# Where the causal mask of the attention scores is added, and how a column of scales is spread over a row: TensorE matmuls in place of a VectorE pass and of transposes

## The reference, cut to what matters

```python
def diff_attention(q, k, v, lam):
    for i in range(S // Q_BLOCK):                     # 8 blocks of 128 queries
        q0 = i * Q_BLOCK
        end = q0 + Q_BLOCK
        s = jnp.einsum('bqhcd,bkhcd->bhcqk', q[:, q0:end], k[:, :end]) * scale
        causal = kpos[None, :] <= qpos[:, None]
        p = jax.nn.softmax(jnp.where(causal, s, -jnp.inf), axis=-1)
        w = p[:, :, 0] - lam * p[:, :, 1]
        outs.append(jnp.einsum('bhqk,bkhe->bqhe', w, v[:, :end]))

def rmsnorm(x, g):
    y = x * lax.rsqrt(jnp.mean(x * x, axis=-1, keepdims=True) + NORM_EPS)
    return y * g
```

## Time and profile before

| what | value |
|---|---|
| median of 3 runs | 3637.75 us (3637.38 to 3641.05) |
| profiled execution, its own time | 3641.05 us |
| its span, first to last instruction | 3639.3 us |
| TensorE busy | 3379.2 us, 93% of the span |
| VectorE, ScalarE, GpSimd busy | 1452.7, 831.0 and 937.0 us |
| mean granted TensorE clock | 0.957 |
| attention with the head 0 projections left out | about 305 to 949 us of the span |
| dilated attention | about 1780 to 2370 us |

### The profile page before, as it was taken

How to read it: one execution, slowest core, us unless ns; L and a number is a source line. 1 busy time by engine, 2 the same in 40 slices (tenths; PEclk the granted TensorE clock), 3 DMA queues, 4 the chain that set the end, 5 groups by cost and what they waited for, 6 DMA issues and landing times.

```text
span 3639.3 us, 41501 instructions
## 1 busy us (share of the span) xinstructions
PE 3379.2 (93%) x15810; PEld 2742.8 (75%) x15810; DVE 1452.7 (40%) x1896; ACT 831.0 (23%) x1308; POOL 937.0 (26%) x514
## 2 busy tenths in 40 slices
PE   6989999998797898989999999889999989999999
PEld 5767777776685676768788888768787768888887
DVE  5653545455555666640021223222611542323231
ACT  4442333333201322221122222211201020101010
POOL 2222111110131221113222222234233323333332
PEclk9999999998898899979999999999999989999999
DMA  2110000000255012101211212231112111111112
GB/s 103 46 36 30 30 30 24 30 24 18 79 181 202 29 59 70 47 24 47 96 50 56 64 47 71 64 116 58 41 46 67 71 35 47 46 52 46 52 46 75
DMA packets 83698, 214.10 MB, mean 59 GB/s; under 512 B 7024, under 2 KB 33264, under 8 KB 83456
## 3 DMA queue, kind: packets, MB, share of 16 engines
q1 hardware_dynamic: 48176, 167.27, 14.1%
q10 hardware_dynamic: 35408, 45.24, 4.0%
HBM read 193.44 MB, written 19.04 MB: 58 GB/s over the span
## 4 chain that ended last, share of the span: by engine, by line
PE 80%; DVE 12%; ACT 3%; issue 3%; DMA 1%; PEld 1%; ACTq 0%; DVEq 0%; PEldq 0%; POOL 0%; SPq 0%; POOLq 0%
PE proj_bank L208 21%; PE proj_bank L210 20%; PE proj_bank L209 20%; PE aux_banks L208 2%; PE aux_banks L209 2%; PE aux_banks L210 2%; PE aux_banks L690 2%; PE aux_banks L1727 1%; ACT att_p L797 1%; PE aux_banks L699 1%; PE aux_banks L1410 1%; PE aux_banks L754 1%; DVE aux_banks L866 1%; PE aux_banks L1751 1%; PE aux_banks L495 1%
## 5 line engine op out<-in xcount | busy, mean ns | idle before, releaser
L208 PE MATMUL proj_bank<-h_hi,slab_hi 128*128 128x512 f32 x2816 | 1128.6, 401 | 41.9 <-ACT att_q L788 12.4
L209 PE MATMUL proj_bank<-h_lo,slab_hi 128*128 128x512 f32 x2816 | 1108.6, 394 | 0.0
L210 PE MATMUL proj_bank<-h_hi,slab_lo 128*128 128x512 f32 x2816 | 1108.6, 394 | 0.0
L226 POOL CAST slab_hi<-slab_raw 128x1024 fp32r<-128x1024 f32 x255 | 270.7, 1061 | 2659.7 <-PE proj_bank L210 2373.0
L228 POOL TENSOR_TENSOR slab_lo<-slab_raw,slab_hi 128x1024 fp32r<-128x1024 f32 x255 | 666.5, 2614 | 20.4
L208 PEld LDWEIGHTS proj_bank<-h_hi,slab_hi 128*128 128x128 f32 x2816 | 537.0, 191 | 168.3 <-issue 20.9
L210 PEld LDWEIGHTS proj_bank<-h_hi,slab_lo 128*128 128x128 f32 x2816 | 536.0, 190 | 115.2
L209 PEld LDWEIGHTS proj_bank<-h_lo,slab_hi 128*128 128x128 f32 x2816 | 537.2, 191 | 109.6 <-issue 2.2
L208 PE MATMUL proj_bank<-ffn_hi,slab_hi 128*128 128x512 f32 x512 | 199.2, 389 | 0.0
L209 PE MATMUL proj_bank<-ffn_lo,slab_hi 128*128 128x512 f32 x512 | 199.2, 389 | 0.0
L210 PE MATMUL proj_bank<-ffn_hi,slab_lo 128*128 128x512 f32 x512 | 199.2, 389 | 0.0
(11 more groups left out here) (329 smaller groups left out, 4099.2 us busy)
## 6 DMA issues: line engine op xcount, KB each, us to landing
slab_raw<-wts SPq DMA_DIRECT2D x255, 512.0 KB, 3.3
ada_w<-ada_w SPq DMA_DIRECT2D x64, 384.0 KB, 3.2
ssd_decay_rows<-decay_sums ACTq DMA_DIRECT2D x16, 512.0 KB, 4.2
dil_rows<-dilated_out ACTq DMA_DIRECT2D x12, 520.0 KB, 8.3
x_first<-xT SPq DMA_DIRECT2D x4, 1024.0 KB, 9.1
x_again<-xT ACTq DMA_DIRECT2D x4, 1024.0 KB, 8.1
x_kept<-x ACTq DMA_DIRECT2D x8, 512.0 KB, 4.3
mix_kept<-ssd_mix ACTq DMA_DIRECT2D x8, 512.0 KB, 7.7
```

The costliest lines, as they stand in the source:

```text
L208: pe.matmul(bank, k.whi[:, slot, wk, :], hi[:, xk, cols], start=first and a == 0, stop=False)
L209: pe.matmul(bank, k.whi[:, slot, wk, :], lo[:, xk, cols], start=False, stop=False)
L210: mm = pe.matmul(bank, k.wlo[:, slot, wk, :], hi[:, xk, cols], start=False, stop=last and a == len(ks) - 1)
L226: pool.tensor_copy(k.whi[:, slot], k.raw[:, slot]).then_inc(k.s_hi, 1)
```

## The change

Two edits. First, the mask is added by TensorE: behind each component's last score matmul a bfloat16 matmul of the identity with the 128x128 triangle accumulates into the same 128 columns, and `maxima` becomes one plain maximum over all keys for each component, each waiting for its own component only. Second, the spreads are no longer transposes but plain float32 matmuls with the same two operands. The mask operand shrinks to a bfloat16 copy of identity and triangle.

```diff
@@ make_core
-    k.mask = at("mask_row", 28.75, [P, MASK_W], BF16)
+    k.mask = at("mask_operands", 28.25, [P, 2, P], BF16)
@@ rstd_stage (line 282); the same edit in lines 717, 1148 and 1734
-            mm = pe.transpose(k.aux[:, bank0 + j // 4, (j % 4) * P:(j % 4 + 1) * P],
-                              k.rstd[:, j:j + 1].to_broadcast([P, P]), k.ident)
+            mm = pe.matmul(k.aux[:, bank0 + j // 4, (j % 4) * P:(j % 4 + 1) * P],
+                           k.rstd[:, j:j + 1].to_broadcast([P, P]), k.ident, start=True, stop=True)
@@ vectors_stage
-        dve.memset(k.mask[:, 0:MASK_W - P], 0.0)
-        dve.tensor_copy(k.mask[:, MASK_W - P:], k.causal)
+        dve.tensor_copy(k.mask.rearrange("p a b -> p (a b)"), k.const[:, IDENT:CAUSAL + P])
@@ attention_stage
-    mx = k.small[:, 64:68]
+    mx = k.small[:, 64:66]
@@ scores
-                mm = pe.matmul(own, q, kt[rows, par, i * P:keys], start=True, stop=True)
+                pe.matmul(own, q, kt[rows, par, i * P:keys], start=True, stop=False)
+                mm = pe.matmul(own, k.mask[:, 0], k.mask[:, 1], start=False, stop=True)
@@ maxima
-            early = max(0, keys - MASK_W)
             flat = score.rearrange("p (c a) b -> p c (a b)", c=2)
-            if early:
-                dve.wait_ge(s_score, step * 2 + 2)
-                v.settle(dve, dve.tensor_reduce(mx[:, 0:2], flat[:, :, 0:early], AX, ALU.max))
-                dve.sem_inc(s_seen, 1)
             for c in range(2):
-                if not early:
-                    dve.wait_ge(s_score, step * 2 + (c + 1))
-                    dve.sem_inc(s_seen, 1)
-                own = flat[:, c, early:keys]
-                ins = dve.tensor_tensor_reduce(own, own, k.mask[:, MASK_W - (keys - early):], 1.0, mx[:, c:c + 1] if early else LOWEST,
-                                               ALU.add, ALU.max, mx[:, 2 + c:3 + c])
+                dve.wait_ge(s_score, step * 2 + (c + 1))
+                ins = dve.tensor_reduce(mx[:, c:c + 1], flat[:, c, 0:keys], AX, ALU.max)
             v.settle(dve, ins)
-            dve.tensor_scalar(nmax, mx[:, 2:4], -SCALE, None, ALU.mult).then_inc(s_nmax, 1)
+            dve.tensor_scalar(nmax, mx, -SCALE, None, ALU.mult).then_inc(s_nmax, 1)
```

More of the change, by code:

```diff
@@ L28 @@
 NEG = -1e30
-LOWEST = -3e38
-MASK_W = 5 * 128
 ADA = 6 * D
@@ L123, in at @@
     def at(name, kb, shape, dt=F32):
-        size = (2 if dt == BF16 else 4) * int(np.prod(shape[1:]))
+        size = 4 * int(np.prod(shape[1:]))
         assert kb * 1024 + size <= k.top, (name, kb, size)
@@ L620, in attention_stage @@
     nmax, total, inv, lr = (k.small[:, 48 + 4 * i:50 + 4 * i] for i in range(4))
-    mx = k.small[:, 64:68]
+    mx = k.small[:, 64:66]
     score, turn, out = k.aux[:, 0:4, :], k.aux[:, 4, :], k.aux[:, 5, :]
     s_evac = k.sem("att_evacuated")
-    s_score, s_seen = k.sem("att_scored"), k.sem("att_scores_seen")
+    s_score = k.sem("att_scored")
     s_nmax = k.sem("att_max")
@@ L716, in spread @@
             for j in range(4):
-                mm = pe.transpose(turn[:, j * P:(j + 1) * P], k.rstd[:, 4 * a + j:4 * a + j + 1].to_broadcast([P, P]), k.ident)
+                mm = pe.matmul(turn[:, j * P:(j + 1) * P], k.rstd[:, 4 * a + j:4 * a + j + 1].to_broadcast([P, P]),
+                               k.ident, start=True, stop=True)
             mm.then_inc(s_turned, 1)
@@ L944, in _ @@
         with dve.Fori(0, (HEADS - 2) // 2) as m:
-            v.enter(m, 2 * (TT * 4 + 3))
+            v.enter(m, 2 * TT * 4)
             for b in range(2):
@@ L1147, in _ @@
             for j in range(TT):
-                mm = pe.transpose(k.aux[:, 2 * g + j // 4, (j % 4) * P:(j % 4 + 1) * P],
-                                  rstd[:, g * TT + j:g * TT + j + 1].to_broadcast([P, P]), k.ident)
+                mm = pe.matmul(k.aux[:, 2 * g + j // 4, (j % 4) * P:(j % 4 + 1) * P],
+                               rstd[:, g * TT + j:g * TT + j + 1].to_broadcast([P, P]), k.ident, start=True, stop=True)
             mm.then_inc(s_b, 1)
@@ L1733, in spread @@
             for b in range(TT):
-                mm = pe.transpose(spread_banks[:, b * P:(b + 1) * P], rstd[:, TT + b:TT + b + 1].to_broadcast([P, P]), k.ident)
+                mm = pe.matmul(spread_banks[:, b * P:(b + 1) * P], rstd[:, TT + b:TT + b + 1].to_broadcast([P, P]), k.ident, start=True, stop=True)
             mm.then_inc(s_spread, 1)
```

## The result

The changed kernel takes 3702.53 us (median of 4 runs, 3698.24 to 3704.24) against 3639.4 us of the kernel before in the same comparison: ratio 1.017, 95% interval 1.0152 to 1.0187. It is slower by about 63 us; the forecast was 3647.0, range 3636 to 3660. Its profiled execution took 3699.84 us and has a span of 3698.0 us, 58.7 more than before.

What follows compares the result with a forecast made beforehand. TensorE, busy for 93% of the span, was taken as the bound. Terms 10.8 + 5.5 + 0.9 - 5.8 - 2.1 = +9.3 us on the median 3637.75 gave 3647.0, range 3636 to 3660.

Steps and rivals of the forecast that it cites:

- the part on the mask: Attention scores: 128 new one-pass mask matmuls on TensorE at 0.06 us each, range 0.057 to 0.115.
- switching number format is dear: Rival, attention: each mask waits out the matmul ahead and costs 0.27 us, kernel at 3667; chance 0.10.
- The dilated spreads, +10.8: Dilated attention, 12 heads: eight spreads each gain a second record that nothing covers, 0.90 us a head, 10.8 us more.
- The norms, +5.5: Four norms of `rstd_stage`: 1.7 us more each for three, 0.4 behind block 1 where a DMA wait hides the rest.
- the state space norm, +0.9: Norm of the state space output: VectorE waits only for the first eight spreads, 0.9 us more.
- Spreads of the attention, 6 x 0.45 + 1.7 = 4.4: Attention: spreads as matmuls cost 0.45 us a head in heads 1 to 6 and 1.7 at head 7's end.
- The relief, 17.5: Attention: plain maxima, the first running while TensorE scores the second component, shorten the chain; 17.5 us less.
- the forecast case: Whole kernel: the summed terms without clock recovery, 3647.0 us, own range 3642 to 3653; chance 0.54.
- the clock recovers: Rivals, TensorE's clock in the attention: recovered in part, 3637, chance 0.20; wholly, 3628, chance 0.06.
- The waits of steps 6 and 7: Attention heads 1 to 6: TensorE's waits for the weights, 0.96 and 0.81 us, both go; -1.77 a head.

Runs made afterwards that it cites:

- e3: Changed kernel with spreads back as transposes and both mask matmuls issued behind both components' scores; 3631.67 us, ratio 0.9977 to the kernel before.
- e10: Changed kernel with spreads back as transposes and only the second component's mask, behind both components' scores; 3609.91 us, ratio 0.9928 to the kernel before.
- e6: Changed kernel with spreads back as transposes and both masks ahead of both components' scores, diagonal block first; 3610.63 us, ratio 0.9922 to the kernel before.
- e2: Changed kernel with spreads back as transposes, so mask and maxima edit alone; 3672.94 us, ratio 1.0089 to the kernel before.
- e5: Changed kernel with spreads back as transposes and no mask matmuls, so the plain maxima alone; 3617.0 us, ratio 0.9935 to the kernel before.
- e4: Changed kernel with spreads back as transposes and masks contracting over the component's own 64 rows only; 3638.61 us, ratio 0.9999 to the kernel before.
- e1: Kernel before with only the spreads as plain float32 matmuls; 3659.76 us, ratio 1.0053 to the kernel before.
- e7: Kernel before with the score matmuls alternating between the two components; 3621.53 us, ratio 0.9951 to the kernel before.
- e11: Kernel before with each component's diagonal block scored ahead of its other parts; 3623.6 us, ratio 0.9961 to the kernel before.
- e8: Changed kernel with spreads back as transposes, both masks ahead of the scores, and components' parts alternating; 3607.8 us, ratio 0.9907 to the kernel before.

## Why the prediction was wrong

**The step that failed** is in the part on the mask: "128 new matmuls (8 heads, 8 steps, 2 components), one pass, 128 columns", costed at 0.06 us each, with "Nothing is below 0.057" and 0.115 as the upper bound. It took the price of the new instruction and left out what its place does to its neighbours. In e3 and e10, where the mask stands behind both components, it costs 0.05 and 0.04 us of TensorE's time, and in e6 two masks in a row start 0.056 us apart: the price was right. Between the components it costs the overlap of 64-row matmuls as well: 56 us for the 128 of them (e2 minus e5). The evidence lay in the trace of before: the scores of step 3, 512 columns of float32 for each component, took 1.07 us for both. A float32 record of 128 columns costs 0.112 us in a sequence, so one component's four blocks with two records each are 0.9 us and both 1.8; 1.07 is possible only side by side. I had not priced the scores from the records, only the instruction that was added.

The rival *switching number format is dear* also put a loss in the attention, 3667, but by another mechanism; e4 shows that the mechanism is wrong.

**Point by point.**
- *The dilated spreads, +10.8.* From the first to the last k product of the stage it is 524.8 us before, 536.0 in e1 and 533.8 in the changed kernel: +11.2 and +9.0 for eleven of the twelve heads, where the forecast had 9.9. The first head grows from 47.2 to 48.1. Right. VectorE's wait before that product in the first head is 6.60 us against 5.69.
- *The norms, +5.5, and the state space norm, +0.9.* VectorE waits 3.74 us for the spread of the first norm instead of 2.06, 1.7 as forecast, and behind block 1 the wait for the DMA shrank from 1.26 to 0.84 us only, so that this spread cost 1.4 us from the reciprocal to the sum and not 0.4. At the state space norm VectorE waits 3.27 us, against 1.24 before: +2.0 and not 0.9, since the records there take 0.17 us each (31 in 5.33 us) and I had counted full clock. Outside the attention all terms together are 18.3 against 17.2; misses of both signs are in it.
- *Spreads of the attention, 6 x 0.45 + 1.7 = 4.4.* In e1 the attention takes 647.5 us, +3.2. Right in kind and nearly in size.
- *The relief, 17.5.* Larger: the attention of e5 is 23.7 us shorter than before, 2.0 in head 0, 16.1 in heads 1 to 6 and 5.6 in head 7 and its norm. Its places and its mechanism were right. VectorE in step 6 of head 2 of e5, with TensorE's last scores and the instruction behind them:

```profile
505.73 2.09 DVE L855 TENSOR_REDUCE small<-aux_banks 128x1 f32<-128x896 f32 x2 [1.01 <-PE aux_banks L690]
506.27 0.38 PE L690 MATMUL aux_banks<-att_k,att_q 64*128 64x128 f32 x2
506.59 0.44 PE L696 MATMUL aux_banks<-const,att_p 128*128 128x128 f32 x2
507.85 0.17 DVE L857 TENSOR_SCALAR small<-small 128x2 f32<-128x2 f32 x1
```

The first component's maximum does run while TensorE scores the second, and the scaling starts 1.2 us behind the last score, against 2.7 before: 1.5 less, as forecast. In step 7 it is 1.5 less for a forecast 1.7, and in steps 1, 2 and 4, where both components are ready together, the weights come 0.27 us earlier and not 0.1. What was short is the gain of TensorE. From its scores of step 6 to those of step 7 it takes 11.47 us before and 10.29 in e5, and from there to the next head's 12.31 and 11.27. That is 2.2 us a head, where the idle times of the two waits add up to 1.77: idle time is counted from the end of the last record, 0.27 us behind its start, while in a sequence the next record starts 0.11 behind it, which is 0.3 of the 0.45. Heads 1 to 6 have also two short stretches at half clock in e5 and three before, some 2 us less.
- *The clock.* In head 7 and its norm the granted clock is 0.77 before (851 to 949 us), 0.77 in the changed kernel (889 to 993) and 0.76 in e1 (854 to 955), where only the spreads became matmuls; the other transposes of head 7 stayed what they were in all three. No recovery, as the forecast case had it, and nothing for *the clock recovers*.
- *The waits of steps 6 and 7* are gone in the changed kernel too. TensorE's waits in heads 1 to 6 there:

```profile
PE aux_banks L697 <- issue: 3.5, 2, 1.7
PE aux_banks L687 <- issue: 2.4, 2, 1.4
PE aux_banks L697 <- DVE att_o L890: 1.0, 6, 0.2
```

Of the 3.6 us a head 0.2 is left: TensorE became the limit almost everywhere, with longer scores. The kernel loses 58.7 and not the 55.6 of its halves. Longer spreads that no longer fall into waits are not the reason: in the attention they add 3.2 us to the kernel before (e1) and 2.6 to e2. The 3 us lie outside it, and within what the intervals leave open.

## What to carry to other kernels

Before an instruction is put between two others, ask what these two do together: here matmuls on 64 rows each ran side by side, over the last four records of the first group, and one over all 128 rows between the groups cost the kernel 0.44 us instead of 0.05 of TensorE's time. A group whose records times their mean length is well above the time it occupies is overlapping; compare the number of records in a merged row with its length before you price a neighbour. An instruction that only accumulates can go ahead of such a pair or behind it. Neither is free: ahead it cost TensorE 0.10 us, behind it 0.05, but there it also held back the engine that could have started on the first half (e3, 15 us over e5). Splitting work in equal alternating parts extends the overlap.

## What the runs showed that was not expected

VectorE's last instruction of the weights in step 6 got faster without being touched. The groups by shape for it, first the kernel before, then e5 (records, busy us, mean ns):

```profile
L877 DVE SCALAR_TENSOR_TENSOR att_p<-att_p,small 128x896 f32<-128x896 f32 x8 | 13.8, 1724 | 0.3
```

```profile
L865 DVE SCALAR_TENSOR_TENSOR att_p<-att_p,small 128x896 f32<-128x896 f32 x8 | 9.2, 1151 | 0.3
```

In the kernel before it starts while GpSimd casts a weight slab; in e5 it starts earlier and is done before GpSimd begins. Timeline of e5:

```profile
511.42 1.15 DVE L865 SCALAR_TENSOR_TENSOR att_p<-att_p,small 128x896 f32<-128x896 f32 x1
...
512.67 1.04 POOL L224 CAST slab_hi<-slab_raw 128x1024 fp32r<-128x1024 f32 x1 [17.35 <-PE proj_bank L208]
...
513.67 0.60 PE L696 MATMUL aux_banks<-const,att_p 128*128 128x128 f32 x4
```

The collision is no part of the relief, though. In e7 and e11 it is still there (1.80 us in heads 0 to 6), and both are faster than the kernel before. And in e5 TensorE starts on these weights 1.1 us after they are ready, so 0.65 us more would not have held it up; the shorter maxima had already taken the wait away.

Overlap with GpSimd does not by itself slow VectorE. In e3 the cast starts while this instruction runs:

```profile
513.45 1.15 DVE L866 SCALAR_TENSOR_TENSOR att_p<-att_p,small 128x896 f32<-128x896 f32 x1
513.64 1.86 POOL L224 CAST slab_hi<-slab_raw 128x1024 fp32r<-128x1024 f32 x1 [17.41 <-PE proj_bank L208]
```

VectorE needs its 1.15 us, and it is the cast that takes 1.86 instead of 1.04; e6 and e8 show the same (1.43 and 1.76 in this head). In the kernel before the cast had begun 0.26 us ahead of VectorE, and VectorE took 1.80. So of these two the one that starts second is the one that gets longer, and which it is depends on when TensorE frees the slab. No run moved the cast alone.
